# Attention stage: the turns of a pair's weights, the outputs one pair back and the next scores are issued as one group per pair of steps

## The reference, cut to what matters

```python
s = einsum('bhgqd,bhnd->bhgqn', qb, k_cmp) * scale        # compressed keys, 15 of them
p_cmp = masked_softmax(s, cmp_end <= t)
o_cmp = einsum('bhgqn,bhnd->bhgqd', p_cmp, v_cmp)
...                                                       # 4 blocks of 64 keys, all of them chosen
p = masked_softmax(einsum('bhgqd,bhqkd->bhgqk', qb, ks) * scale, smask)
o_sel = einsum('bhgqk,bhqkd->bhgqd', p, vs)
...
p = masked_softmax(einsum('bhgqd,bhkd->bhgqk', qb, kw) * scale, wmask)
o_win = einsum('bhgqk,bhkd->bhgqd', p, vw)
o = einsum('bsch,cbshd->bshd', sigmoid(g_br), [o_cmp, o_sel, o_win])
y_attn = o.reshape(B, S, Q_COLS) @ w_attn_out
```

## Time and profile before

| | |
|---|---|
| median of 3 runs | 747.46 us (746.82 to 747.47) |
| span of the profiled execution, first to last instruction | 745.2 us |
| own time of the profiled execution | not printed by itself; the runs lie 1.6 to 2.3 us above the span |
| TensorE busy, weight loads busy | 740.4 us, 641.4 us |
| VectorE, ScalarE, GpSimd busy | 518.0, 416.4, 66.5 us |
| granted TensorE clock over the span | 1.000 |
| attention stage | about 75 to 222 us of the span |

### The profile page before, as it was taken

The page is one execution under the profiler, slowest core; times in us unless marked ns, Lnnn a source line. Parts: engine busy times, 40 slices in busy tenths (PEclk is TensorE's granted clock), DMA queues, the critical chain, the costliest instruction groups (busy, mean ns, idle before and its releaser), DMA issues.

```text
span 745.2 us, 11582 instructions
## 1 busy us (share of the span) xinstructions
PE 740.4 (99%) x4563; PEld 641.4 (86%) x4563; DVE 518.0 (70%) x834; ACT 416.4 (56%) x788; POOL 66.5 (9%) x103
## 2 busy tenths in 40 slices
PE   9999999999999999999999999999999999999998
PEld 8999999877888888888888888887888888888886
DVE  5784677885756678887367757898667777447762
ACT  5575557556463455565356546597646656345640
POOL 6300000000010000430000004400100000000000
PEclk9999999999999999999999999999999999999999
DMA  8998444343455546766656461735355655656611
GB/s 266 297 311 274 85 109 153 114 128 123 146 170 197 167 152 222 198 213 228 188 172 212 171 226 54 251 124 174 111 168 170 191 204 174 222 170 188 207 57 56
DMA packets 99209, 131.26 MB, mean 176 GB/s; under 512 B 5357, under 2 KB 79163, under 8 KB 99156
## 3 DMA queue, kind: packets, MB, share of 16 engines
q1 hardware_dynamic: 96564, 125.58, 52.6%
q0 software_dynamic: 2304, 4.43, 2.7%
q10 hardware_dynamic: 288, 0.52, 0.2%
HBM read 128.68 MB, written 1.84 MB: 175 GB/s over the span
## 4 chain that ended last, share of the span: by engine, by line
PE 97%; DVE 2%; ACT 1%; issue 0%; POOL 0%; POOLq 0%
PE B L1626 39%; PE B L1592 22%; PE B L1597 11%; PE B L1581 11%; PE B L1805 2%; PE B L1852 2%; PE B L1815 2%; PE B L1639 1%; PE B L1685 1%; PE B L1633 1%; DVE LO L1002 1%; PE B L1808 1%; PE B L1832 1%; PE B L1730 1%; PE B L1791 0%; PE B L1729 0%
## 5 line engine op out<-in xcount | busy, mean ns | idle before, releaser
L1002 DVE TENSOR_TENSOR LO<-RAW,HI 128x1024 fp32r<-128x1024 f32 x236 | 282.5, 1236 | 101.0 <-ACT HI L538 100.5
L1626 PE MATMUL B<-HI,AA 128*128 128x512 f32 (+1 forms) x960 | 286.8, 376 | 0.3 <-DVE AA L1008 0.2
L538 ACT ACTIVATE HI<-RAW 128x1024 fp32r<-128x1024 f32 (+1 forms) x240 | 237.2, 1038 | 63.1 <-PE B L1626 58.2
L1626 PEld LDWEIGHTS B<-HI,AA 128*128 128x128 f32 x960 | 175.7, 188 | 33.8 <-issue 1.6
L1592 PE MATMUL B<-AA,HI 128*128 128x512 f32 x704 | 179.2, 393 | 0.0
L1626 PE MATMUL B<-LO,AA 128*128 128x512 f32 (+1 forms) x480 | 178.6, 372 | 0.0
L1592 PEld LDWEIGHTS B<-AA,HI 128*128 128x128 f32 x704 | 126.8, 189 | 23.0 <-issue 0.7
L1626 PEld LDWEIGHTS B<-LO,AA 128*128 128x128 f32 x480 | 90.6, 189 | 14.6
L1597 PEld LDWEIGHTS B<-AA,LO 128*128 128x128 f32 x704 | 96.6, 190 | 7.1
L1597 PE MATMUL B<-AA,LO 128*128 128x256 f32 x704 | 98.8, 282 | 0.0
L1581 PE MATMUL B<-AA,HI 128*128 128x256 f32 x448 | 83.3, 287 | 0.0
(11 more groups left out here) (313 smaller groups left out, 634.9 us busy)
## 6 DMA issues: line engine op xcount, KB each, us to landing
RAW<-in_w_in SPq DMA_DIRECT2D x29, 1024.0 KB, 5.8
RAW<-in_w_gate SPq DMA_DIRECT2D x22, 1024.0 KB, 5.3
RAW<-in_w_up SPq DMA_DIRECT2D x22, 1024.0 KB, 5.3
RAW<-in_w_down SPq DMA_DIRECT2D x22, 1024.0 KB, 5.0
RAW<-in_w_in SPq DMA_DIRECT2D x10, 512.0 KB, 6.4
RAW<-in_w_attn_out SPq DMA_DIRECT2D x4, 1024.0 KB, 5.1
RAW<-in_w_o SPq DMA_DIRECT2D x4, 1024.0 KB, 5.0
RAW<-in_w_out SPq DMA_DIRECT2D x4, 1024.0 KB, 5.0
```

What stands on the lines that cost most here:

```text
L538: e.activation(pieces(HI, NSPL, i, k), pieces(RAW, NRAW, i, k), ACT.Copy).then_inc(split_hi, 1)
L1002: e.tensor_tensor(pieces(LO, NSPL, i, k), pieces(RAW, NRAW, i, k), pieces(HI, NSPL, i, k), ALU.subtract).then_inc(split_lo, 1)
L1626: x = e.matmul(dst, a, w[:, t, c0:c0 + n], start=(first and t == 0 and k == 0), stop=(last and t == nk - 1 and k == 2))
```

## The change

TensorE's loop over places is reordered. A list `rounds` holds the pairs and the compressed steps, a list `places` the places where they begin and the place after the last. At each such place TensorE now issues together: the turns of both steps of the round before, the outputs of the round before that, and the scores that begin there; the filler pieces of the place follow. At the places between there is only filler. The last outputs come at place 27, ahead of its filler piece. The programs of the other engines are the same.

```diff
+        rounds = [[b] if b in CMP else [b, b + 1] for b in begins]
+        places = begins + [NSTEP]
...
-                if i < NSTEP:
-                    scores(i)
+                if i in places:
+                    m = places.index(i)
+                    if m >= 1:
+                        for s in rounds[m - 1]:
+                            turn_weights(s)
+                    if m >= 2:
+                        for s in rounds[m - 2]:
+                            outputs(s)
+                    if i < NSTEP:
+                        scores(i)
+                if i == NSTEP + 1:
+                    for s in rounds[-1]:
+                        outputs(s)
                 for _ in range(FILL_AT[i]):
                     next(filler)
-                if 1 <= i <= NSTEP:
-                    turn_weights(i - 1)
-
-                if i >= 2 and i - 2 in CMP:
-                    outputs(i - 2)
-                if i >= 3 and i - 3 in begins and i - 3 not in CMP:
-                    outputs(i - 3)
-                    outputs(i - 2)
```

## The result

The changed kernel takes 773.21 us in the median of 5 runs (767.97 to 773.42) against 746.82 (5 runs beside it) before: ratio 1.033, 95% interval 1.032 to 1.035, +26.4 us. Forecast were 766.4 us and a range of 761 to 771. The direction and the place were right, the size was not: 6.8 us are missing in the forecast.

The account below looks back on a forecast made before the run. TensorE was taken to bound the kernel: waits of 19.5 us less 0.6 for switching give +18.9, so the span goes from 745.2 to 764.1; with 2.3 between span and median, 766.4 us, range 761 to 771.

Parts of the forecast that it names:

- What bounds the kernel: Whole span: TensorE, busy 740.4 of 745.2 us, sets the end, so every microsecond it waits is added to the time.
- The chain of VectorE: Pair 9, 10: from scores to second weights VectorE is busy 8.55 of 8.86 us in fixed order; TensorE can't shorten it.
- The waits: TensorE's moved turns wait for VectorE's weights, at pairs' second steps and compressed steps 2 and 13: 19.5 us in sum.
- The rule that the second turn's new place is the first turn's old start: Each pair: the wait is the end of the second weights less the time where the first turn starts today.
- The allowance of 0.15 us: Added to each wait as an estimate for semaphore and first weight load on TensorE.
- Next to no saving from grouping: TensorE: a turn costs the same anywhere; saved switching is 0.6 us, between 0 and 1.5.
- The two groups fewer: One TensorE group goes at each compressed step, 2 and 13, saving at most 0.3 us of switching twice.
- the clock: Rival: TensorE's clock falls to about half pace in the waits, costing up to about 3 us each time; chances 0.15, 0.05.
- If it happened at the longest wait (4.2 us): Clock rival with one fall, at compressed step 13: 769.5 us, chance 0.15.
- If at all four waits of 3 us or more: Clock rival with falls at all four such waits: 778.5 us, chance 0.05, left out of the range.
- The argument set against it: Against the clock rival: dense stretches of 6 us and more between waits, and all waits but one 3 us or less.
- 2.3 us between span and time: Median of runs, 747.46, lies 2.3 above the profiled span of 745.2; this was added to the forecast span of 764.1.

Follow-up runs that it names:

- Experiment 4: Changed kernel with ScalarE's exponents and VectorE's weights of both steps of every pair done together, ahead of filler work: 758.48 us, ratio 1.016.
- experiment 5, the second kernel: Kernel before with pairs' second turns behind the first's, and both steps' exponents and weights together for pairs 5, 9, 14, 18, 20, 22, 24: 747.82 us, ratio 1.0012.
- the first: Changed kernel with exponents and weights together for pairs 5, 9, 14, 18, 20, 22, 24, and compressed steps' weights ahead of the splits: 753.75 us, ratio 1.009.
- the run with the short idle work: Changed kernel plus idle matmuls ahead of four waits, 11 each at steps 2, 6, 10 and 16 at 13: 766.57 us, ratio 1.026.
- the run with the long idle work: Changed kernel plus idle matmuls ahead of four waits, 24 each at steps 2, 6, 10 and 36 at 13: 776.65 us, ratio 1.041.

## Why the prediction was wrong, step by step

**What bounds the kernel**: right. TensorE had no slack, and each wait showed in the end.

**The chain of VectorE**: right. The pair 9, 10 after the change, on VectorE:

```profile
138.68 1.29 DVE L1138 TENSOR_REDUCE SM<-B 128x2 f32<-128x512 f32 x2 [5.83 <-PE B L1811]
139.88 2.35 DVE L1005 TENSOR_TENSOR LO<-RAW,HI 128x1024 fp32r<-128x1024 f32 x2
...
145.12 1.22 DVE L1005 TENSOR_TENSOR LO<-RAW,HI 128x1024 fp32r<-128x1024 f32 x1
...
146.84 0.69 DVE L1159 TENSOR_TENSOR PR<-PR,SM 128x512 f32<-128x512 f32 x1
```

From 138.68 to 146.84 + 0.69 = 147.53 it is 8.85 us, before 8.86, with the same operations; TensorE's turn starts at 147.58. Experiment 4 shows it by taking the filler work out of the chain.

**The waits**: forecast 6.1 for steps 6 and 10, measured 5.84; 3.0 and 4.2 for 2 and 13, measured 2.94 and 4.15; 3.6 for 19 and 21, measured 3.55; 1.3 for 15, measured 1.65; 0.7, 0.45 and 0.15 for 23, 25 and 1, measured 0.66, 0.40 and about 0.1 (in no row of waits: the eight transposes of pair 0 at 83.99 last 1.15 us, an unhindered eight 1.04). Sum 19.5 forecast, 19.2 measured and the 0.1. The rule that the second turn's new place is the first turn's old start held. The allowance of 0.15 us was too large (the turn of step 10 starts 0.05 us behind VectorE); at 15, 19 and 21 it offsets waits that came out longer than the rest of their sums, so part of the close agreement is luck.

**Next to no saving from grouping**: right to within what was measured. The turns next to each other save nothing (experiment 5, the second kernel). The two groups fewer show in the first: at full clock it lies 4.3 to 5.3 us above the kernel before, with 5.3 us of idle time in its three waits, so what they save is between 0 and 1 us; 0.6 was forecast, and it can't be told closer.

**The step that failed is the clock.** The sum of the forecast, 19.5 less 0.6, has no term for it: it stands only among the rivals, and there its weight was wrong. "If it happened at the longest wait (4.2 us): 766.4 + 3 = 769.5. If at all four waits of 3 us or more: 766.4 + 12 = 778.5 ... For the one, 0.15; for all, 0.05." It happened at three of the four in the profiled run, for 7.1 us. The rival's mechanism and its price of one fall, up to 3 us, were right (2.7, 2.8 and 1.6 measured); its chance was not, and the cases between one fall and four were left out altogether. The argument set against it, that dense stretches lie between the waits and that only one wait is longer than 3 us, has no row behind it: no wait of that length was in the trace. The rule of the Trainium skill that I set beside it ("TensorE: Matmul & The Clock Gate", The HAM clock gate: an idle TensorE goes to half clock until it has been busy again) was the better guide. This trace agrees with it in part: 0.50 granted behind three waits, but 1.00 behind the one of 2.75 us, and at step 13 the fall came when TensorE was busy again.

In spans the forecast was 764.1 us and the measured one 771.5; of these 7.4 us the clock is 7.1. I put 2.3 us between span and time where it is 1.7 (773.21 over 771.5), which hid 0.6 of the miss. With most of the falls kept out the kernel runs at 765.3 to 767.3 us, and its profiled span of 765.5 still holds one fall. That its median, 766.57, lies 0.2 us from the forecast of 766.4 is in part luck: the 0.6 us raised the forecast, and falls like that one raise the measured time.

## What to carry to other kernels

Where one engine is never idle, an instruction may be moved forward only as far as its producer's own chain allows, and that chain is read from the producer's timeline between two events that it can't pass: here VectorE did other work between the two halves of a pair. Price the wait, and then the clock: here waits of 2.9 us on a dense TensorE cost nearly as much again in the instructions behind them, 2.7 and 2.8 us, where the clock fell, and small matmuls of no use, issued while it waited, took most of that part away (4.2 of some 7 us in the medians). Count them by the instructions they become, since too many are added to the time in full. Before an order is changed on one engine, change the orders of those that feed it; here even that only gives back the kernel before, since grouping itself brought nothing.

## What the runs showed of the hardware that was not expected

- The clock falls at waits that a trace calls short, and not at each of them: where TensorE had stood idle for 2.79, 2.79 and 3.99 us, not after 2.75; in the run with the short idle work behind a wait of 1.78 us, and not behind one of 1.63 us thirteen microseconds earlier. In the run with the long idle work the same wait at step 21, again 1.78 us, left the clock at 1.00. Two kernels with waits of 2.5 and 3.7 us, and of 2.5 and 2.5 us, had runs with no fall and with some. So the length of the wait alone does not decide it.
- A fall can come after the wait: 0.47 us behind its end at step 13 of the changed kernel, and 0.88 us behind that of 1.78 us, with TensorE busy in between.
- The falls make the time of one kernel spread: 768.0 to 773.4 us in nine runs of the changed one, against 746.0 to 748.1 in thirteen runs of the kernel before. What decides in a run where the falls come was not tried.
- A fall costs the group behind it a factor of 1.8 (5.41 against 2.95 us for 31 small matmuls), and it ended by itself after at most 6.2 us of busy work in the changed kernel's profiled run.
